# Differential attention scores as whole-array products, with query and key parts laid out on both partition halves

## The reference

```python
def diff_attention_branch(q, k, v, z, cos, sin, lam_params, subln_w, lambda_init):
    q = partial_rope(q.reshape(bsz, seq, DIFF_HEADS, 2, DIFF_DH), cos, sin) * (DIFF_DH ** -0.5)
    k = partial_rope(k.reshape(bsz, seq, DIFF_HEADS, 2, DIFF_DH), cos, sin)
    ...
    def attend(q_blk):
        s = jnp.einsum('nbhqd,nbhkd->nbhqk', q_blk, k).astype(f32)
        p = jax.nn.softmax(s, axis=-1)
        a = p[0] - lam * p[1]
        return jnp.einsum('bhqk,bhkd->bhqd', a.astype(v.dtype), v)
    ...
    o = rmsnorm(o, subln_w) * (1.0 - lambda_init)
    return o * jax.nn.silu(z)
```

## Time and profile before

| | |
|---|---|
| median of three runs | 3000.14 us (2998.05 to 3001.43) |
| the profiled execution | 2999.76 us, of which 2998.0 us are its span |
| granted TensorE clock | 0.995 of full speed over the span |
| TensorE matmul, busy | 2950.4 us, 98% |
| VectorE, busy | 1730.1 us, 58% |
| ScalarE, busy | 1437.7 us, 48% |
| GpSimd, busy | 464.8 us, 16% |
| L2554, the score matmuls | 384, in two stretches between 516.0 and 1642.4 us |

### The profile page before, as it was taken

The page is one execution under the profiler, slowest core; times in us unless marked ns, Lnnn a source line. Parts: engine busy times, 40 slices in busy tenths (PEclk is TensorE's granted clock), DMA queues, the critical chain, the costliest instruction groups (busy, mean ns, idle before and its releaser), DMA issues. The chain is left out here.

```text
span 2998.0 us, 51224 instructions
## 1 busy us (share of the span) xinstructions
PE 2950.4 (98%) x20500; PEld 2370.3 (79%) x20500; DVE 1730.1 (58%) x2626; ACT 1437.7 (48%) x2817; POOL 464.8 (16%) x293
## 2 busy tenths in 40 slices
PE   9999999999999999999999999999999999999999
PEld 7788788777787887877777877778888777788887
DVE  7767743676537677635676456564444555544443
ACT  4555543666434555534665355653223357632322
POOL 2555530000013445410000030000000100000000
PEclk9999999999999999999999999999999999999999
DMA  4121122212222112122221222122222222122222
GB/s 153 65 75 56 64 75 90 75 61 75 85 83 92 65 65 86 38 91 74 74 76 59 93 103 95 64 73 98 98 98 98 84 75 78 46 102 98 85 97 84
DMA packets 42693, 243.26 MB, mean 81 GB/s; under 512 B 6832, under 2 KB 7792, under 8 KB 17136
## 3 DMA queue, kind: packets, MB, share of 16 engines
q1 hardware_dynamic: 42480, 240.30, 22.6%
HBM read 233.36 MB, written 2.20 MB: 79 GB/s over the span
## 5 line engine op out<-in xcount | busy, mean ns | idle before, releaser
L322 PE MATMUL bank<-hT,ws 128*128 128x512 f32 x2112 | 879.6, 417 | 9.8 <-PEq L1228 6.9
L326 PE MATMUL bank<-hT,ws 128*128 128x512 f32 x2112 | 828.8, 392 | 0.0
L325 PE MATMUL bank<-hT,ws 128*128 128x512 f32 x2112 | 826.7, 391 | 0.0
L273 ACT ACTIVATE ws<-raw 128x2048 fp32r<-128x2048 f32 x172 | 329.0, 1913 | 301.3 <-PE bank L322 188.1
L322 PEld LDWEIGHTS bank<-hT,ws 128*128 128x128 f32 x2112 | 398.9, 189 | 93.7 <-issue 15.9
L326 PEld LDWEIGHTS bank<-hT,ws 128*128 128x128 f32 x2112 | 397.8, 188 | 87.4
L325 PEld LDWEIGHTS bank<-hT,ws 128*128 128x128 f32 x2112 | 399.4, 189 | 68.5 <-issue 3.0
L279 DVE TENSOR_TENSOR ws<-raw,ws 128x2048 fp32r<-128x2048 f32 x154 | 359.1, 2332 | 149.5 <-ACT ws L273 146.1
L279 POOL TENSOR_TENSOR ws<-raw,ws 128x2048 fp32r<-128x2048 f32 x18 | 88.9, 4937 | 776.8 <-ACT ws L273 776.8
L1273 PE MATMUL bank<-uS,ws 128*128 128x512 f32 x512 | 199.2, 389 | 0.0
L1276 PE MATMUL bank<-uS,ws 128*128 128x512 f32 x512 | 199.2, 389 | 0.0
(11 more groups left out here) (407 smaller groups left out, 4795.9 us busy)
## 6 DMA issues: line engine op xcount, KB each, us to landing
raw<-in_w_ff SPq DMA_DIRECT2D x64, 1024.0 KB, 4.7
raw<-in_w_delta SPq DMA_DIRECT2D x32, 1024.0 KB, 4.7
raw<-in_w_diff SPq DMA_DIRECT2D x32, 1024.0 KB, 4.7
raw<-in_w_att SPq DMA_DIRECT2D x20, 1024.0 KB, 4.8
raw<-in_w_merge_a SPq DMA_DIRECT2D x16, 1024.0 KB, 4.7
raw<-in_w_merge_b SPq DMA_DIRECT2D x16, 1024.0 KB, 4.7
raw<-in_w_out SPq DMA_DIRECT2D x16, 1024.0 KB, 4.8
rows<-sum_rows SPq DMA_DIRECT2D x16, 512.0 KB, 5.6
```

Source lines behind the costliest of these rows:

```text
L273: act.activation(self.k.ws[:, c % 2, 0], self.k.raw[:, c % 2], ACT.Copy).then_inc(self.high_done, 1)
L322: first = pe.matmul(out, hi, x[:, 0, k], start=(begin and k == steps[0]), stop=False)
L325: pe.matmul(out, hi, x[:, 1, k], start=False, stop=False)
L326: last = pe.matmul(out, lo, x[:, 0, k], start=False, stop=(end and k == steps[-1]))
```

## The change

The two maps of a head get whole-array operands. Of the query, `QS` holds for each map its high part on that map's 64 partitions and its low part on the other 64. Of the key, `KH` holds the high part of a map on both halves and `KL` the low part on both halves. Then one matmul on 128 partitions gives high·high + low·high, and a second one high·low + low·low (a term that the kernel before leaves out). A unit has four such matmuls in place of six on half the partitions, and map 0 is finished before map 1 begins.

Who fills the buffers: ScalarE writes the high parts, half by half (two instructions for one). VectorE writes the query's low part into a scratch row of `gt` (two halves), and the key's low part in four half instructions, the last two of which read one half of the partitions and write the other. SyncE then places, with DMAs of 64x512, the query's low part (`place_query`, two) and the second copy of the key's high part (`place_key`, two), between the swap of k and the next weight load. TensorE waits for them before the first unit of a head.

Orders move with it: on ScalarE `qk_high_part` stands ahead of `raw_copy`, and `z_gate` ahead of `v_turned`; on VectorE `qk_low_part` stands ahead of `norm_out` and `weights`; at the start of the phase the first scores come after `turn_v` and eight more fill steps. `AT` moves into unused rows of `gt`, `O` into `cg`, so that `cg`, a table of the gated delta phase, is loaded again between the two layers (in `out_phase`, behind `pA` and ahead of the next weight chunks on SyncE's queue).

```diff
+def diff_phase(k, st, following, lam, yS, odd, gt, cg, angles=()):
...
@@ -2436,12 +2436,16 @@
...
-        qk = k.sb(ctx, "qk", [P, 2, 2, 2, SEQ], F32R)
+        ql = gt[:, 0].bitcast(F32R)
+        QS = k.sb(ctx, "q_high_and_low", [P, 2, 2, SEQ], F32R)
+        KH = k.sb(ctx, "k_high_twice", [P, 2, 2, SEQ], F32R)
+        KL = k.sb(ctx, "k_low_twice", [P, 2, 2, SEQ], F32R)
+        MAPS = (slice(0, 64), slice(64, P))
...
-        AT = k.sb(ctx, "AT", [P, 2, SEQ], F32)
-        O = k.sb(ctx, "O", [P, NTOK, P], F32)
+        AT = gt[:, GATES_AHEAD_B:GATES_AHEAD_B + 2]
+        O = Carve(cg, F32)(NTOK, P)
...
@@ -2464,11 +2468,24 @@
                     if h == 0:
                         sp.wait_ge(cleared, 1)
                     else:
-                        sp.wait_ge(qk_ready, nth(h - 1, 2, j))
+                        sp.wait_ge(qk_mixed, nth(h - 1, 2, j))
...
+                def place_query(h):
+
+                    sp.wait_ge(qk_ready, nth(h, 2, 0))
+                    for m in range(2):
+                        sp.dma_start(QS[MAPS[1 - m], h % 2, m].bitcast(F32), ql[MAPS[m]].bitcast(F32)).then_inc(query_placed, 16)
+
+                def place_key(h):
+
+                    sp.wait_ge(key_high, h + 1)
+                    sp.dma_start(KH[MAPS[1], h % 2, 0].bitcast(F32), KH[MAPS[0], h % 2, 0].bitcast(F32)).then_inc(key_placed, 16)
+                    sp.wait_ge(qk_high, nth(h, 2, 1))
+                    sp.dma_start(KH[MAPS[0], h % 2, 1].bitcast(F32), KH[MAPS[1], h % 2, 1].bitcast(F32)).then_inc(key_2_placed, 16)
...
@@ -2480,11 +2497,15 @@
                 refill(0, 1)
                 swap(0, 0)
                 swap(0, 1)
+                place_query(0)
+                place_key(0)
                 refill(1, 0)
                 for h in range(1, HEADS):
                     swap(h, 0)
                     refill(h, 1)
                     swap(h, 1)
+                    place_query(h)
+                    place_key(h)
                     if h + 1 < HEADS:
                         refill(h + 1, 0)
...
@@ -2546,15 +2567,15 @@
                     h, n = head(u)
                     if n == 0:
                         pe.wait_ge(qk_ready, nth(h, 2, 1))
+                        pe.wait_ge(query_placed, 32 * (h + 1))
                     if u > 0:
                         pe.wait_ge(p_ready, 2 * u)
-                    for t, (a, b) in enumerate(((0, 0), (0, 1), (1, 0))):
-                        for m in range(2):
-                            hp = slice(64 * m, 64 * (m + 1))
-                            last = pe.matmul(B[SB + m][:, :], qk[hp, h % 2, 0, a, n * P:(n + 1) * P], qk[hp, h % 2, 1, b],
-                                             start=(t == 0), stop=(t == 2))
-                            if t == 2:
-                                last.then_inc(s_ready, 1)
+                    for m in range(2):
+                        if n == 0:
+                            pe.wait_ge((key_placed, key_2_placed)[m], 16 * (h + 1))
+                        q = QS[:, h % 2, m, n * P:(n + 1) * P]
+                        pe.matmul(B[SB + m][:, :], q, KH[:, h % 2, m], start=True, stop=False)
+                        pe.matmul(B[SB + m][:, :], q, KL[:, h % 2, m], start=False, stop=True).then_inc(s_ready, 1)
...
@@ -2581,10 +2602,10 @@
 
                 fill = stream()
                 some(fill, 3 * KT + 4)
-                scores(0)
-                some(fill, KT - 4)
                 turn_v(0)
                 some(fill, KT)
+                scores(0)
+                some(fill, 4)
...
@@ -2629,7 +2650,12 @@
 
                 def qk_high_part(h, j):
                     act.wait_ge(qk_mixed, nth(h, 2, j))
-                    act.activation(qk[:, h % 2, j, 0], rq[:, j], ACT.Copy).then_inc(qk_high, 1)
+                    for m, hp in enumerate(MAPS):
+                        ins = act.activation((QS, KH)[j][hp, h % 2, m], rq[hp, j], ACT.Copy)
+                        if m == 1:
+                            ins.then_inc(qk_high, 1)
+                        elif j == 1:
+                            ins.then_inc(key_high, 1)
...
@@ -2663,21 +2689,21 @@
                 raw_copy(0, 0)
                 raw_copy(0, 1)
                 st.high(act, 1, 0)
+                qk_high_part(0, 0)
                 raw_copy(0, 2)
-                qk_high_part(0, 0)
                 qk_high_part(0, 1)
+                v_turned(0)
+                z_gate(0)
                 exps(0)
-                z_gate(0)
-                v_turned(0)
                 for u in range(UNITS1):
                     h, n = head(u)
                     more = h + 1 < HEADS
+                    if n in (1, 2) and more:
+                        qk_high_part(h + 1, n - 1)
                     if n < 3 and more:
                         raw_copy(h + 1, n)
                     elif not more:
                         gate_copy(n)
-                    if n in (1, 2) and more:
-                        qk_high_part(h + 1, n - 1)
                     if n == 0 and more:
                         st.high(act, h + 1, 1)
                     if u + 1 < UNITS1:
@@ -2696,8 +2722,8 @@
                         following.first_high(act, st)
                     if n == 3:
                         if more:
+                            z_gate(h + 1)
                             v_turned(h + 1)
-                            z_gate(h + 1)
                         if h > 0:
                             high_part(h - 1)
...
@@ -2717,7 +2743,17 @@
 
                 def qk_low_part(h, j):
                     dve.wait_ge(qk_high, nth(h, 2, j))
-                    dve.tensor_tensor(qk[:, h % 2, j, 1], rq[:, j], qk[:, h % 2, j, 0].bitcast(F32), ALU.subtract).then_inc(qk_ready, 1)
+                    if j == 0 and h > 0:
+                        dve.wait_ge(query_placed, 32 * h)
+                    for m, hp in enumerate(MAPS):
+                        low = KL[hp, h % 2, m] if j else ql[hp]
+                        ins = dve.tensor_tensor(low, rq[hp, j], (QS, KH)[j][hp, h % 2, m].bitcast(F32), ALU.subtract)
+                        if m == 1 and j == 0:
+                            ins.then_inc(qk_ready, 1)
+                    if j == 1:
+                        for m, hp in enumerate(MAPS):
+                            ins = dve.tensor_tensor(KL[MAPS[1 - m], h % 2, m], rq[hp, 1], KH[hp, h % 2, m].bitcast(F32), ALU.subtract)
+                        ins.then_inc(qk_ready, 1)
...
@@ -2757,10 +2793,10 @@
                 if angles:
                     dve.wait_ge(turned, len(angles))
                 mix(0, 0)
+                st.low(dve, 1, 0)
+                qk_low_part(0, 0)
                 mix(0, 1)
-                qk_low_part(0, 0)
                 qk_low_part(0, 1)
-                st.low(dve, 1, 0)
                 maxes(0)
                 weights(0)
                 for u in range(UNITS1):
@@ -2770,6 +2806,8 @@
                         maxes(u + 1)
                     if n == 0 and more:
                         st.low(dve, h + 1, 1)
+                    if n in (1, 2) and more:
+                        qk_low_part(h + 1, n - 1)
                     if n == 1 and h > 0:
                         norm_out(h - 1)
                     if u + 1 < UNITS1:
@@ -2778,8 +2816,6 @@
                         following.second_low(dve)
                     if n < 2 and more:
                         mix(h + 1, n)
-                    if n in (1, 2) and more:
-                        qk_low_part(h + 1, n - 1)
...
+                    diff_phase(k, s_diff, s_mb, lam, yS, odds(), gt, cg[:, :], () if l else (k.sin1, k.cos1))
...
-                            out_phase(k, s_out, s_next, mS, macc[:, 0:2], OUT_BANKS_MERGE, KT - 1, [(pA, a["pA"][l + 1])],
+                            out_phase(k, s_out, s_next, mS, macc[:, 0:2], OUT_BANKS_MERGE, KT - 1, [(pA, a["pA"][l + 1]), (cg[:, :], a["cg"])],
```

More of the change, by code:

```diff
@@ L2410, in diff_stream @@
     return Stream(k, 2, HEADS, w, l)
-def diff_phase(k, st, following, lam, yS, odd, gt, angles=()):
+def diff_phase(k, st, following, lam, yS, odd, gt, cg, angles=()):
     nc = k.nc
@@ L2421, in diff_phase @@
         "max_ready", "exp_ready", "weights_ready", "weights_turned", "weights_t_ready", "o_ready")
-    osq, orms, on_ready, yt_ready, yhi, ylo, step, astep, cleared, qk_mixed, qk_high, turned = k.sems(
+    osq, orms, on_ready, yt_ready, yhi, ylo, step, astep, cleared, qk_mixed, qk_high, turned, query_placed, key_placed, key_2_placed, key_high = k.sems(
         "o_square", "o_rms", "o_normed", "y_t_ready", "y_high_done", "y_low_done", "diff_step", "diff_act_step",
-        "rotation_cleared", "qk_mixed", "qk_high_done", "angles_ready")
+        "rotation_cleared", "qk_mixed", "qk_high_done", "angles_ready", "query_placed", "first_key_placed", "second_key_placed", "first_key_high")
     B, ps = k.bank, k.ps
@@ L3702, in build @@
                     gated_merge_phase(k, s_ma, s_diff, yS, macc, gt)
```

(2 more changed lines are left out.)

## The result

| | before | changed |
|---|---|---|
| median of 12 runs | 3000.61 us (2993.4 to 3003.58) | 3006.63 us (3002.6 to 3010.58) |
| ratio, 95% interval | | 1.0023 [1.0015, 1.0031] |
| the profiled execution | 2999.76 us, span 2998.0, granted clock 0.995 | 3002.6 us, span 3000.8, granted clock 0.997 |

The change costs 6.0 us (4.5 to 9.3 by the interval) where 3.4 us of gain were forecast, and 3006.63 lies 0.6 us above the range. The two profiles are only 2.8 us apart, but the granted clock of the one of before is 0.002 lower, and 0.002 of 3000 us is some 6 us.

What follows compares the result with a forecast made beforehand. The prediction took TensorE, busy 98%, as the bound: -8.6 us gain, +4.5 us stalls for L279, +0.7 us reload of `cg`, so -3.4 us against 2999.76, giving 2996.4 us; range (8 in 10) 2990.5 to 3006.

Steps and rivals of the forecast that it cites:

- TensorE's gain: Edges around a unit's score matmuls go: 0.135 us less a unit, 0.54 a head, 8.6 us over 64 units.
- Rival 3: Six score matmuls are worth three slots and the edges stay: four slots cost 14.5 us more, 3014.3 us; chance 0.07.
- The mechanism: Helpers' loop takes 32.22 us a head, TensorE needs 31.72; TensorE waits for VectorE's L279 at n = 3, 4.5 us in all.
- Two half copies of 0.63 us ... I take the same overlap of 0.08: ScalarE's two halves of the query's high part in the helpers' loop: 0.55 us each from start to start.
- Four half subtractions of 0.61: VectorE's four half instructions for the key's low part, ending at 20.45 us of the helpers' loop.
- an edge of its range: Half instructions without the 0.08 us overlap: loop grows by 0.56 us, d is 1.06, stalls 10 us, time 3001.9 us.
- The growth rule 5d - 0.3: TensorE's stalls per phase when L279's lateness grows by d a head, head 1 starting 0.3 late: 2.25 us.
- Rival 2: Subtractions reading one half and writing the other cost twice the price: stalls 16.6 us, 3008.5 us; chance 0.15.
- The reload of `cg`: Between the layers, the reload delays a weight load by 2.5 us, and TensorE's product by 0.7 us; bounds 0 and 10.2.
- rival 1: Helpers' loop is under 31.8 us (30.2 with halves at half price), TensorE never waits: 2991.2 to 2992 us; chance 0.28.
- the time at d = 0.35: Lower end of the main case, L279's lateness growing by 0.35 us a head: 2994 us.
- Theory C: Explanation tested in the follow-up runs, not in the prediction: the time is lost outside this phase.

Runs made afterwards that it cites:

- one_key_low: The changed kernel with the key's low part standing once, read by both maps, without VectorE's two subtractions from half to half: 2996.1 us, ratio 0.9991 to the kernel before.
- before_halves: The kernel before, with the high and low parts of q and k made in two instructions of 64 partitions each: 3006.57 us, ratio 1.0022 to the kernel before.

## Why the prediction failed

- **TensorE's gain was right:** 0.51 us a head against 0.54, 8.2 us against 8.6. The products of a unit take about 0.01 us longer in all. Rival 3 is out.
- **The mechanism was right:** the helpers form one loop that no longer waits for TensorE, and TensorE waits for L279 in n = 3. The swap of k is exposed (0.62 us of wait), with 4.07 us as taken.
- **The step that failed is "Two half copies of 0.63 us ... I take the same overlap of 0.08" with "Four half subtractions of 0.61".** Each half on other partitions than the one ahead waits for its end: from start to start 0.65 us on ScalarE and 0.70 on VectorE. Over the links that is 0.70 us net, loop 32.92 in place of 32.22. The prediction priced this as an edge of its range (loop + 0.56, stalls of 10 us, 3001.9) and took the overlap. Its row for a half, is a multiplication, not a subtraction, and tells a duration alone, since a wait stands behind each of the 16. The trace of before had rows that tell the distance: a copy on partitions 64 to 127 takes 0.43 us, and the instruction on all partitions behind it, which waits for nothing, starts after 0.46 (so at 14 of 16 such places):

```profile
1205.24 0.43 DVE L2336 COPY Xf<-bank 64x256 f32<-64x256 f32 x1 [0.38 <-PE bank L1939]
1205.70 0.75 DVE L2224 SCALAR_TENSOR_TENSOR cb<-cb,small 128x512 f32<-128x512 f32 x1
```

- **The growth rule 5d - 0.3 had its offset wrong.** With the measured d of 1.17 it gives 5.6 us a phase; 6.8 were there, since the first two stalls were 0.39 and 0.62 and not 0, and the third already 1.16 (the 0.3 was a choice). Both mis-sizings together: 13.5 us of stalls for 4.5.
- **Rival 2 did not come in its own form.** Reading one half and writing the other costs no more than any half: L2755's pair takes 1.41 us, as L2750's. Its outcome, a kernel that is slower, came by the lost overlaps: the loop grew by 0.70 us of the 1.0 that it asked for.
- **The reload of `cg`** was booked with 0.7 us. ScalarE's wait for the next weight load grew from 3.97 to 5.43 us, 1.46 us in place of the 2.5 taken and less than the 1.8 of cover; no wait of TensorE for that chunk is in the view of its waits there: 0.
- **Not foreseen:** the 2.5 us in the delta phase.
- **Two sums of the prediction are off, and nothing hangs on them:** rival 1's 30.2 us is 29.9 by the terms (32.22 less half of 1.10, 1.18 and 2.44), and the time at d = 0.35 is 2994.8.

The sum by measured terms: -8.2 + 13.5 + 2.5 = +7.8 us; the medians say +6.0, and the interval's 4.5 to 9.3 holds both. The lost overlaps by themselves would have left the time in the range: with d = 1.17 the prediction's own sum gives 3003.0 us. Theory C holds for those 2.5 us only.

## What to carry to other kernels

Where two engines hand work round in a loop beside a saturated one, add up the loop and compare it with the saturated engine's period: any link counts in full, and each period pays the difference; then look for a second way beside the first before pricing a cure, as one_key_low did not. Price a pair of instructions from start to start, on the same partitions as yours, since a split by partitions costs two whole instructions that do not overlap (1.41 us for the pair), and a split by columns almost nothing (0.67). What is free in a steady loop can cost at the start of a phase, where nothing hides it, as the halves in before_halves do.

## What the runs showed of the hardware that was not expected

- A change of partitions from one instruction to the next costs 0.08 to 0.1 us of lost overlap, on ScalarE as on VectorE (0.42 against 0.33 us at 256 columns, 0.65 to 0.70 against 0.52 to 0.61 at 512).
- TensorE ran at the lower clock behind each of two idle times of 4.65 us (granted clock 0.91 and 0.81 in the 18 us around them), and not behind the stalls of 1.16 us (1.00 over both phases of the changed kernel).
- VectorE's 1600th record starts 0.40 to 0.45 us after the wait ahead of it, in place of 0.045, and so do others apart from it by multiples of 128, up to the 2624th. Which instruction falls there depends on how many stand ahead in the program; here it turned who holds the port, 4.80 us in place of 0.74.
